# Turning the first feed-forward products: weights as the loaded operand, high and low token parts as one 512-column moving block

## The chip, the cores and the metric

The kernel runs on one core of one Trainium2 chip. A core has five engines that run side by side and meet only at semaphores: TensorE (PE, matrix products; its weight loads are listed apart as PEld), VectorE (DVE), ScalarE (ACT), GpSimd (POOL) and SyncE (SP, which here only issues transfers). A matrix product loads a 128 x up to 128 block into the array and lets up to 512 columns of another operand move through it; the sums land in PSUM, which has eight banks of 128 x 512 fp32. The metric is the device time of one execution in microseconds, the median of three runs. Less is better.

## The reference, cut to what matters

Two decoder blocks are applied to 256 tokens of width 1024, all in fp32. Between the mixers stand six feed-forward layers: two with a squared ReLU (hidden width 4096) and four gated ones (hidden width 2816).

```
def rms_norm(x, w):
    y = xf * lax.rsqrt(jnp.mean(xf * xf, axis=-1, keepdims=True) + NORM_EPS)
    return (y * w.astype(jnp.float32)).astype(x.dtype)

def squared_relu_mlp(h, w_up, w_down):
    return jnp.square(jax.nn.relu(h @ w_up)) @ w_down

def swiglu(h, w_in, w_out):
    gu = h @ w_in
    gate, up = jnp.split(gu, 2, axis=-1)
    return (jax.nn.silu(gate) * up) @ w_out
...
x = x + squared_relu_mlp(rms_norm(x, mlp_norm[layer]), w_up[layer], w_down[layer])     # twice
x = x + 0.5 * swiglu(rms_norm_2(x, ffn_norm[i, j]), ffn_w_in[i, j], ffn_w_out[i, j])   # four times
```

The factor rsqrt(...) of rms_norm is one number per token. It can be applied to the product `h @ w` afterwards.

## The kernel before, in words

**Products.** Every large product is done in three fp32r passes: an operand is split into a high part (rounded) and a low part (the rest), and high x high, high x low and low x high are summed in PSUM. The weights come from memory as panels of 128 x 2048 fp32 (1 MB) through a ring of four buffers `raw`; SP issues the load of panel q+4 when the low part of panel q has been made. ACT makes `w_hi` of a panel in two halves (`split`, L1427), DVE makes `w_lo` (L2001), in two buffers each. `multiply` (L611 to L613) is the three passes; it waits for `lo_ready` of each half panel, and counts `w_used` when a panel is done, which frees its buffers for the panel after the next.

**First feed-forward product before.** The transposed tokens `h_hi`, `h_lo` (128 of the 1024 inputs on the partitions, 256 tokens) are the loaded operand, in blocks of 128 tokens; 512 columns of weights move. So the result of a block of 512 hidden units has tokens on the partitions: two PSUM banks, one for each 128 tokens (`tt`). A block is two panels, thus 48 matmuls of 512 columns. There are 8 blocks in a squared-ReLU layer ("mlp"), 11 in a gated layer ("ffn"; a block is 256 gate and 256 up columns), 60 in all, with 2880 such matmuls.

**What follows a block.** ACT evacuates the banks with the token's norm factor `rstd` as a scale on the partition (L1483, ReLU; L1486, SiLU), DVE squares (L2064) or multiplies gate and up (L2070) into `tm`. The second product needs hidden units on the partitions, so PE transposes `tm` (`hidden_t`, `transpose_batch`, L625): 8 blocks of 128 x 128 for an mlp block, 4 for an ffn block, between the two panels of the next block. ACT and DVE split the transposed result into `hid_hi` (L1492) and `hid_lo` (L2077). The second product (`hid_hi`, `hid_lo` loaded, `w_down` moving) adds into `x_sb` (`residual`, L2034).

**Entering a layer.** `enter` does the first block in pieces: first half of panel 0, then `norm_batch` (transposes of the second half of `x_sb`, L625), second half, and after `t_lo` says that the second half of `h_lo` is there, panel 1. Meanwhile ACT sums squares (L1450) and POOL makes `rstd` (L2719, L2721); ACT goes on to the panels of block 1 only behind that.

The order on each engine is the order of the code; the loops over blocks (`Fori`) hold two blocks each before.

## Time and profile before

| | |
|---|---|
| time, median of 3 runs (lowest, highest) | 1735.3 us (1735.07, 1736.16) |
| profiled execution: its own time, its span | 1737.58 us, 1735.8 us |
| PE busy, PEld busy | 96%, 78% |
| DVE busy, ACT busy, POOL busy | 55%, 48%, 4% |
| mean granted TensorE clock | 0.99 |
| HBM | 167 GB/s over the span |

The three runs lie within 1.1 us. The time of an execution is 1.8 us more than its span (first to last recorded instruction). "Busy" of PE counts matmuls from their start to a modelled end, and they overlap: a 512-column matmul is listed with some 390 ns although the next begins 227 ns later. So what a matmul costs is read from the distance between starts, here called its pitch, or from the chain of waits, and not from its duration. For ACT and DVE, which work one instruction after another, the listed duration is the cost; two alike in a row are a little cheaper (a pair of DVE splits is 2.36 us, one alone 1.22).

### The profile page before, as it was taken

Reading aid. Unit: us, or ns where it says so; the run is one execution under the profiler, and the core shown is the slowest. Engines: PE = TensorE matmul, PEld = TensorE weight load, DVE = VectorE, ACT = ScalarE, POOL = GpSimd, SP = SyncE. Lnnn points to the kernel's source line nnn. Section 1 sums busy time; section 2 is a strip of 40 time slices with the busy share of each in tenths; the row PEclk is TensorE's granted clock in tenths of the full one; section 3 lists DMA queues with packets and bytes.
Section 4 is the critical chain, followed back from the end, with each engine's and each line's share of the span. In section 5 each row is a group of like instructions: output and inputs, shape, how many; then the busy total and the mean of one; then the engine's idle time right before and its main releaser. Section 6 shows DMA issues by size and latency. Waiting matters only on the chain.

```text
span 1735.8 us, 23226 instructions
## 1 busy us (share of the span) xinstructions
PE 1667.9 (96%) x8978; PEld 1359.5 (78%) x8978; DVE 962.3 (55%) x1250; ACT 840.4 (48%) x1213; POOL 75.5 (4%) x96
## 2 busy tenths in 40 slices
PE   6998999999999999799999999999999999899997
PEld 5778788887767888688888878888878888568886
DVE  4766565446765554455555565554555544465544
ACT  4742454344764543354445535444454435554433
POOL 1313000001000000000001000000000000000000
PEclk9999999999999999899999999999999999999999
DMA  7330444565213455445557544555545555235552
GB/s 260 127 117 22 175 170 170 197 220 223 98 50 128 172 185 194 157 171 189 176 199 270 177 148 185 191 174 193 212 162 182 194 195 193 73 122 193 185 193 83
DMA packets 41166, 291.75 MB, mean 168 GB/s; under 512 B 4832, under 2 KB 4992, under 8 KB 6528
## 3 DMA queue, kind: packets, MB, share of 16 engines
q1 hardware_dynamic: 39968, 282.75, 45.2%
q0 software_dynamic: 1120, 7.88, 1.4%
q8 instruction: 58, 0.95, 0.2%
q14 instruction: 20, 0.16, 0.0%
HBM read 289.56 MB, written 1.05 MB: 167 GB/s over the span
## 4 chain that ended last, share of the span: by engine, by line
PE 90%; DVE 5%; ACT 3%; issue 1%; DMA 0%; POOL 0%; SPq 0%; POOLq 0%; DVEq 0%; ACTq 0%
PE ps L611 26%; PE ps L613 25%; PE ps L612 25%; PE ps L625 3%; PE ps L965 2%; DVE w_lo L2001 1%; DVE gd_c L2304 1%; PE ps L777 1%; PE ps L778 1%; PE ps L779 1%; ACT w_hi L1427 1%; PE ps L1264 1%; DVE h_lo L2014 1%; PE ps L1250 0%; PE ps L842 0%
## 5 line engine op out<-in xcount | busy, mean ns | idle before, releaser
L2001 DVE TENSOR_TENSOR w_lo<-raw,w_hi 128x1024 fp32r<-128x1024 f32 x516 | 607.6, 1219 | 431.0 <-ACT w_hi L1427 427.1
L1427 ACT ACTIVATE w_hi<-raw 128x1024 fp32r<-128x1024 f32 x516 | 510.8, 1040 | 467.5 <-PE ps L613 442.2
L611 PE MATMUL ps<-w_hi,h_hi 128*128 128x512 f32 x1328 | 531.8, 400 | 16.6 <-DVE w_lo L2001 11.0
L613 PE MATMUL ps<-w_hi,h_lo 128*128 128x512 f32 x1328 | 520.9, 392 | 0.0
L612 PE MATMUL ps<-w_lo,h_hi 128*128 128x512 f32 x1328 | 520.1, 392 | 0.0
L611 PEld LDWEIGHTS ps<-w_hi,h_hi 128*128 128x128 f32 x1328 | 251.2, 189 | 73.7 <-issue 14.6
L613 PEld LDWEIGHTS ps<-w_hi,h_lo 128*128 128x128 f32 x1328 | 251.0, 189 | 53.9
L612 PEld LDWEIGHTS ps<-w_lo,h_hi 128*128 128x128 f32 x1328 | 251.6, 189 | 49.6 <-issue 0.5
L611 PE MATMUL ps<-w_hi,hid_hi 128*128 128x512 f32 x672 | 263.0, 391 | 0.0
L613 PE MATMUL ps<-w_hi,hid_lo 128*128 128x512 f32 x672 | 261.6, 389 | 0.0
L612 PE MATMUL ps<-w_lo,hid_hi 128*128 128x512 f32 x672 | 261.5, 389 | 0.0
L611 PEld LDWEIGHTS ps<-w_hi,hid_hi 128*128 128x128 f32 x672 | 126.2, 188 | 26.6 <-issue 0.9
L613 PEld LDWEIGHTS ps<-w_hi,hid_lo 128*128 128x128 f32 x672 | 126.1, 188 | 26.3
L612 PEld LDWEIGHTS ps<-w_lo,hid_hi 128*128 128x128 f32 x672 | 126.2, 188 | 25.6
L2077 DVE TENSOR_TENSOR hid_lo<-ps,hid_hi 128x512 f32 (+3 forms) x60 | 50.1, 834 | 151.6 <-ACT hid_hi L1492 151.6
L1492 ACT ACTIVATE hid_hi<-ps 128x512 f32 (+3 forms) x60 | 42.7, 712 | 188.7 <-PE ps L625 188.7
L1437 ACT ACTIVATE h_hi<-ps,norm_t 128x256 fp32r<-128x256 f32 x88 | 34.5, 475 | 70.1 <-PE ps L625 70.1
L2014 DVE SCALAR_TENSOR_TENSOR h_lo<-ps,norm_t,h_hi 128x256 fp32r<-128x256 f32 x88 | 36.5, 477 | 54.0 <-ACT h_hi L1437 54.0
L2719 POOL TENSOR_SCALAR ms<-ss 128x2 f32<-128x2 f32 x13 | 2.5, 191 | 1290.0 <-ACT junk L1450 1290.0
L625 PE MATMUL ps<-const,tm 128*128 128x128 f32 x304 | 42.9, 272 | 0.0
L625 PEld LDWEIGHTS ps<-const,tm 128*128 128x128 f32 x304 | 36.5, 140 | 8.0 <-DVE tm L2070 0.6
L2070 DVE SCALAR_TENSOR_TENSOR tm<-ps,rstd,tm 128x256 f32<-128x256 f32 x88 | 38.3, 477 | 2.2 <-ACT tm L1486 2.2
(302 smaller groups left out, 1164.7 us busy)
## 6 DMA issues: line engine op xcount, KB each, us to landing
raw<-in_stream SPq DMA_DIRECT2D x266, 1024.0 KB, 4.8
ns_w<-in_ns_w POOLq DMA_DIRECT2D x1, 4096.0 KB, 16.1
ln_rows<-in_ln_rows POOLq DMA_DIRECT2D x2, 1024.0 KB, 10.1
const<-in_const SPq DMA_DIRECT2D x1, 1044.0 KB, 14.3
x_sb<-in_x SPq DMA_DIRECT2D x2, 512.0 KB, 7.7
out<-x_sb SPq DMA_DIRECT2D x2, 512.0 KB, 3.1
row<-in_fin_rows SPq DMA_DIRECT2D x1, 512.0 KB, 18.8
row<-in_fin_rows POOLq DMA_DIRECT2D x1, 512.0 KB, 4.1
```

The costliest lines, as they stand in the source:

```text
L611: pe.matmul(bank[tt], a_hi[:, k_at + k, rows], hi, start=(k == 0), stop=False)
L612: pe.matmul(bank[tt], a_hi[:, k_at + k, rows], lo, start=False, stop=False)
L613: done = pe.matmul(bank[tt], a_lo[:, k_at + k, rows], hi, start=False, stop=(k == q.kt - 1))
L625: done = pe.transpose(tps[:, f, tt * P:(tt + 1) * P], src(tt, f), ident)
L965: done = pe.matmul(ps[half(c), bank, u * 64:(u + 1) * 64], lhs[half(c), u, :], rhs(c, u), start=(u == 0), stop=True, skip_group_check=True)
L1427: act.activation(w_hi[:, static % 2, part], raw[:, static % RING, part], ACT.Copy).then_inc(hi_ready, 1)
L1437: done = act.activation(h_hi[:, k, :], tps[:, f, :], ACT.Copy, scale=norm_t[:, n, k:k + 1])
L1492: act.activation(hid_hi2[:, bass.ds(b * (f_count * T), f_count * T)], tps[:, 0:f_count, :].rearrange("p f t -> p (f t)"), ACT.Copy).then_i ...
L2001: dve.tensor_tensor(w_lo[:, static % 2, part], raw[:, static % RING, part], w_hi[:, static % 2, part].bitcast(F32), ALU.subtract).then_inc ...
L2014: done = dve.scalar_tensor_tensor(h_lo[:, k, :], tps[:, f, :], norm_t[:, n, k:k + 1], h_hi[:, k, :].bitcast(F32), ALU.mult, ALU.subtract)
L2070: done = dve.scalar_tensor_tensor(gate, bank[tt][:, 256:512], rstd[:, tt:tt + 1], gate, ALU.mult, ALU.mult)
L2077: dve.tensor_tensor(hid_lo2[:, cols], tps[:, 0:f_count, :].rearrange("p f t -> p (f t)"), hid_hi2[:, cols].bitcast(F32), ALU.subtract).the ...
```

## The change

The first product of the six feed-forward layers is turned: `w_hi` and `w_lo` are loaded, and the tokens move. `h_hi` and `h_lo` become one buffer `h_both`, and for each 128 inputs (k) and each 128 hidden units (c) there are now two matmuls: `w_hi` loaded, 512 columns moving (256 tokens high, 256 tokens low), and `w_lo` loaded, 256 columns moving (high). A block is now one panel of 8 x 256 weights (256 hidden units; in ffn 128 gate and 128 up), so there are 16 blocks in an mlp layer and 22 in an ffn layer, 120 in all; the loops hold four. The result has hidden units on the partitions, and `hidden_t` is gone. ACT copies the low sums out of PSUM (`low_part`), DVE adds the high sums (`summed`) and applies the token factor, which now lies along the free axis: it is spread over the partitions once a layer, by POOL (two diagonal 128 x 128 blocks of `rstd`, `rms_diag`), PE (a 256-column product with `neg_ones` behind blocks 0 and 1) and ACT (`rows`, copy to `rms_row`). Squaring, or SiLU and the gate product (`gated`), write `inner`, which is split into `hid_hi` (ACT, `store`) and `hid_lo` (DVE, `low_part`). In ffn only the gate half is scaled before SiLU; the up half's factor is applied at the residual (`rstd_half`). The other hunks rename and merge semaphores, or repack the weights ahead of the launch.

```diff
+            def multiply_turned(q, b, bs, halves=(0, 1)):
+                panel = q.panel + b
+                slot = (q.panel + bs) % 2
+                bank = acc[(q.block + bs) % 2]
+                for s in halves:
+                    if s == 0:
+                        if bs >= 2:
+                            free, before, each = read[q.name]
+                            pe.wait_ge(free, before + each * (b - 1))
...
+                    pe.wait_ge(lo_ready, 2 * panel + s + 1)
+                    for k in range(4 * s, 4 * s + 4):
+                        for c in range(2):
+                            cols = slice(k * T + c * P, k * T + (c + 1) * P)
+                            pe.matmul(bank[c], w_hi[:, slot, cols], h_both[:, :, k, :], start=(k == 0), stop=False)
+                            done = pe.matmul(bank[c][:, 0:T], w_lo[:, slot, cols], h_hi[:, k, :], start=False, stop=(k == 7))
...
@@ enter, PE
                 pe.wait_ge(t_lo, t0 + 1)
+                if q.turned:
+                    multiply_turned(q, 0, 0, halves=(0,))
+                    norm_batch(layer, 1)
+                    multiply_turned(q, 1, 1, halves=(0,))
+                    pe.wait_ge(t_lo, t0 + 2)
+                    multiply_turned(q, 0, 0, halves=(1,))
+                    multiply_turned(q, 1, 1, halves=(1,))
+                    return
@@ hidden_layer, PE
-                def body(b, bs, i):
-                    multiply(up, b, bs, i, 0, h_hi, h_lo)
-                    hidden_t(b - 1)
-                    multiply(up, b, bs, i, 1, h_hi, h_lo)
+                pe.wait_ge(diag_ready, hidden_layers.index(layer) + 1)
+                pe.matmul(ps[:, 4, 0:T], cst("neg_ones"), rms_diag[:, :], start=True, stop=True).then_inc(tps_ready, 1)
+                turns, rest = steps(2, up.blocks)
+                with pe.Fori(0, turns) as i:
+                    for k in range(RING):
+                        multiply_turned(up, 2 + RING * i + k, 2 + k)
@@ hidden_layer, ACT
+                def low_part(b, bs):
+                    bank = 2 * ((up.block + bs) % 2)
+                    act.wait_ge(w_used, up.panel + b + 1)
...
+                    act.activation(tm[:, 0, :].rearrange("p (c t) -> p c t", t=T), two[bank][:, :, T:], ACT.Copy).then_inc(low_sums, 1)
+                def body(b, bs, i, weights):
+                    low_part(b - 1, bs - 1)
+                    weights((0,))
+                    if f_count == 1 and bs > 1:
+                        hidden(b - 1, bs - 1)
+                    weights((1,))
+                    if bs == 1:
+                        rows()
+                    if f_count == 2 or bs == 1:
+                        hidden(b - 1, bs - 1)
+                    store(b - 1, bs - 1)
@@ hidden_layer, DVE
+                def body(b, bs, i, weights):
+                    if bs >= 2:
+                        low_part(b - 2, bs - 2)
+                    summed(b - 1, bs - 1)
+                    if bs >= 2:
+                        scaled(b - 1, bs - 1)
+                        weights((0,))
+                    else:
+                        weights((0, 1))
+                        scaled(b - 1, bs - 1)
+                    if f_count == 1:
+                        gated(b - 1, bs - 1)
+                    if bs >= 2:
+                        weights((1,))
@@ inverse_rms, POOL
+                    pool.tensor_scalar(rstd_half[:, :], rstd[:, :], 0.5, None, ALU.mult)
+                    for tt in range(TT):
+                        done = pool.tensor_scalar(rms_diag[:, tt * P:(tt + 1) * P], ident, rstd[:, tt:tt + 1], -1.0,
+                                                  ALU.mult, ALU.mult)
```

PE, first mlp layer, block 1 into block 2 before: the end of panel 0 of block 1, the transposes of block 0's hidden units, and the start of panel 1.

```order
L611 MATMUL ps<-w_hi,h_hi 128x512
L612 MATMUL ps<-w_lo,h_hi 128x512
L613 MATMUL ps<-w_hi,h_lo 128x512
L625 MATMUL ps<-const,tm 128x128 [waits t_lo,tm_ready]
L625 MATMUL ps<-const,tm 128x128 x7
L611 MATMUL ps<-w_hi,h_hi 128x512 [waits lo_ready]
```

PE, the same layer after, the end of block 1 and the start of block 2:

```order
L652 MATMUL ps<-h_both,w_hi 128x512
L653 MATMUL ps<-h_both,w_lo 128x256
L713 MATMUL ps<-rms_diag,const 128x256 [waits diag_ready]
L716 UNCONDITIONAL_BRANCH
L716 ISA
L648 ISA [waits hid_sum]
L652 MATMUL ps<-h_both,w_hi 128x512 [waits lo_ready]
L653 MATMUL ps<-h_both,w_lo 128x256
```

The eight transposes are gone, three matmuls have become two, and one product for the token factors stands once a layer.

DVE, first mlp layer, between the norm's low parts (L2014) and the loop, before:

```order
L2014 SCALAR_TENSOR_TENSOR h_lo<-ps,norm_t,h_hi 128x256
L2001 TENSOR_TENSOR w_lo<-raw,w_hi 128x1024 [waits hi_ready] x4
L2064 TENSOR_TENSOR tm<-tm 128x1024 [waits act_tm]
L2077 TENSOR_TENSOR hid_lo<-ps,hid_hi 128x1024 [waits t_hi]
```

and after, up to the panel for block 3:

```order
L2077 SCALAR_TENSOR_TENSOR h_both<-ps,norm_t,h_both 128x256
L2140 TENSOR_TENSOR tm<-ps,tm 128x512 [waits low_sums]
L2064 TENSOR_TENSOR w_lo<-raw,w_hi 128x1024 [waits hi_ready] x2
L2147 SCALAR_TENSOR_TENSOR tm<-tm,rms_row 128x512 [waits hid_sum,rows_ready]
L2189 UNCONDITIONAL_BRANCH
L2189 ISA
L2161 ISA [waits t_hi]
L2161 TENSOR_TENSOR hid_lo<-inner,hid_hi 128x512
L2134 REGISTER_ALU
L2137 REGISTER_ALU [waits low_sums]
L2140 TENSOR_TENSOR tm<-ps,tm 128x512 [waits act_tm]
L2147 SCALAR_TENSOR_TENSOR tm<-tm,rms_row 128x512 [waits hid_sum]
```

Before, the splits of two panels stand first. After, the sum of block 0 stands ahead of the split of panel 2, and three steps (L2161, L2140, L2147) ahead of that of panel 3.

## Rows read from the trace of the kernel before

**Rows 1.** The page: granted TensorE clock in tenths, by slice of the span.
```profile
PEclk9999999999999999899999999999999999999999
```

**Rows 2.** The page: the chain that ended last, shares by engine.
```profile
PE 90%; DVE 5%; ACT 3%; issue 1%; DMA 0%; POOL 0%; SPq 0%; POOLq 0%; DVEq 0%; ACTq 0%
```

**Rows 3.** The chain in time order (start, us, what): transposes of two mlp blocks.
```profile
214.61 0.87 PE ps L625 x8
226.41 0.88 PE ps L625 x8
```

**Rows 4.** The chain in ffn00: transposes of two blocks.
```profile
747.72 0.44 PE ps L625 x4
759.09 0.44 PE ps L625 x4
```

**Rows 5.** Timeline, second mlp product (start, us, instruction): first and last of 22 matmuls.
```profile
300.15 0.39 PE L612 MATMUL ps<-w_lo,hid_hi 128*128 128x512 f32 x1
300.15 0.19 PEld L613 LDWEIGHTS ps<-w_hi,hid_lo 128*128 128x128 f32 x1
...
304.91 0.39 PE L612 MATMUL ps<-w_lo,hid_hi 128*128 128x512 f32 x1
```

**Rows 6.** Groups by line (busy us, mean ns, idle before): the hidden transposes.
```profile
L625 PE MATMUL ps<-const,tm 128*128 128x128 f32 x304 | 42.9, 272 | 0.0
```

**Rows 7.** Timeline: 24 fp32r matmuls of 256 columns, 48-column loads; first and last.
```profile
420.49 0.28 PE L1202 MATMUL ps<-h_hi,ns_wg_hi 128*48 128x256 f32 x1
...
423.11 0.28 PE L1204 MATMUL ps<-h_lo,ns_wg_hi 128*48 128x256 f32 x1
```

**Rows 8.** Timeline: the same with 16-column loads; first and last of 24.
```profile
41.51 0.28 PE L918 MATMUL ps<-h_hi,gd_wab_hi 128*16 128x256 f32 x1
...
44.20 0.28 PE L920 MATMUL ps<-h_lo,gd_wab_hi 128*16 128x256 f32 x1
```

**Rows 9.** Timeline: 16 loads of 128 columns for 32-column matmuls; the next load.
```profile
448.53 1.86 PEld L1230 LDWEIGHTS ps<-ns_kct,ns_qt 128*128 128x128 f32 x16 [0.76 <-issue]
...
450.31 0.19 PEld L611 LDWEIGHTS ps<-w_hi,h_hi 128*128 128x128 f32 x1
```

**Rows 10.** The chain in the spatial gating: eight fp32 matmuls of 256 columns.
```profile
1012.51 1.99 PE ps L734 x8
```

**Rows 11.** Groups: ACT and DVE work of the kinds that the change adds.
```profile
L2001 DVE TENSOR_TENSOR w_lo<-raw,w_hi 128x1024 fp32r<-128x1024 f32 x516 | 607.6, 1219 | 431.0 <-ACT w_hi L1427 427.1
L1427 ACT ACTIVATE w_hi<-raw 128x1024 fp32r<-128x1024 f32 x516 | 510.8, 1040 | 467.5 <-PE ps L613 442.2 <-POOL rstd L2721 11.0 <-PE ps L1075 10.8
...
L2070 DVE SCALAR_TENSOR_TENSOR tm<-ps,rstd,tm 128x256 f32<-128x256 f32 x88 | 38.3, 477 | 2.2 <-ACT tm L1486 2.2
...
L1874 ACT ACTIVATE ns_pt<-ps 128x512 f32<-128x512 f32 x24 | 13.8, 597 | 6.2 <-PE ps L1264 6.2
...
L2460 DVE TENSOR_TENSOR gd_xt<-gd_xt,ps 128x512 f32<-128x512 f32 x10 | 6.9, 688 | 3.5 <-PE ps L965 3.5
```

**Rows 12.** Timeline: the last matmul of a panel, and ACT's split that waits for it.
```profile
220.58 0.39 PE L613 MATMUL ps<-w_hi,h_lo 128*128 128x512 f32 x1
...
221.00 2.01 ACT L1427 ACTIVATE w_hi<-raw 128x1024 fp32r<-128x1024 f32 x2 [2.56 <-PE ps L613]
```

**Rows 13.** The chain entering mlp0: PE starts after a wait for DVE.
```profile
196.81 0.14 issue
196.95 0.47 PE ps L611
```

**Rows 14.** Timeline entering mlp0: DVE's split of panel 1, ACT behind rstd.
```profile
199.05 2.35 DVE L2001 TENSOR_TENSOR w_lo<-raw,w_hi 128x1024 fp32r<-128x1024 f32 x2
...
205.77 2.01 ACT L1427 ACTIVATE w_hi<-raw 128x1024 fp32r<-128x1024 f32 x2 [1.09 <-POOL rstd L2721]
```

**Rows 15.** Timeline entering ffn10: a 128 x 128 step of POOL.
```profile
1262.69 0.29 POOL L2847 CAST sb_eye<-const 128x128 bf16<-128x128 f32 x1
```

**Rows 16.** Timeline, first ffn block: ACT loads the SiLU table.
```profile
744.40 1.28 ACT L1486 ACT_TABLE_LOAD   x1
```

More of the change, by code:

```diff
@@ L67, in __init__ @@
         self.name, self.kt, self.blocks = name, kt, blocks
-        self.per = -(-kt // PK)
+        self.turned = name.endswith("_up")
+        self.per = 1 if self.turned else -(-kt // PK)
         self.panel, self.block = panel, block
@@ L531, in steps @@
         def steps(first, blocks):
[L534 to L535 removed]
+            turns = (blocks - first) // RING
+            return turns, first + RING * turns
         EV_ORDER = ((0, 0), (1, 0), (0, 1), (1, 1))
@@ L1475, in hidden_layer @@
                 t0 = at[layer][0] + 2
-                def evacuate(b, bs):
-                    act.wait_ge(w_used, up.panel + up.per * (b + 1))
-                    bank = acc[(up.block + bs) % 2]
-                    for tt in range(TT):
-                        if f_count == 4:
-                            done = act.activation(tm[:, tt, :], bank[tt], ACT.Relu, scale=rstd[:, tt:tt + 1])
-                        else:
-                            done = act.activation(tm[:, tt, 0:256], bank[tt][:, 0:256], ACT.Silu,
-                                                  scale=rstd[:, tt:tt + 1])
-                        done.then_inc(act_tm, 1)
@@ L1503, in hidden_layer, with rows @@
-                body(1, 1, 0)
-                pairs, rest = steps(2, up.blocks)
-                with act.Fori(0, pairs) as i:
-                    for k in range(2):
-                        body(2 + 2 * i + k, 2 + k, i)
-                for b in range(rest, up.blocks):
-                    body(b, b, 0)
+                h0 = hidden_before[layer]
+                n = hidden_layers.index(layer)
+                def rows():
+                    act.wait_ge(tps_ready, batches(layer) + 3)
+                    act.activation(rms_row[:, :], ps[:, 4, 0:T], ACT.Copy).then_inc(rows_ready, 1)
@@ new lines, in up_panel, with down_panel @@
+                def up_panel(b, bs, i):
+                    return lambda halves: split(up, b, bs, i, 0, halves)
+                def down_panel(j):
+                    return lambda halves: split(down, 0, 0, 0, j, halves)
+                body(1, 1, 0, up_panel(2, 2, 0))
+                turns, rest = steps(2, up.blocks - 1)
+                with act.Fori(0, turns) as i:
+                    for k in range(RING):
+                        body(2 + RING * i + k, 2 + k, i, up_panel(3 + RING * i + k, 3 + k, i))
@@ L1510, in hidden_layer @@
+                for b in range(rest, up.blocks - 1):
+                    body(b, b, 0, up_panel(b + 1, b + 1, 0))
+                for j in range(2):
+                    b = up.blocks - 1 + j
+                    body(b, b, 0, down_panel(j))
                 for b in range(down.blocks):
                     for j in range(down.per):
-                        if b == 0 and j == 2:
-                            evacuate(up.blocks - 1, up.blocks - 1)
-                            store_t(up.blocks - 1)
@@ L2024, in residual @@
                 q, b, scale = pending.pop()
+                layer = q.name.split("_")[0]
+                if layer in hidden_layers:
+                    dve.wait_ge(diag_ready, hidden_layers.index(layer) + 1)
                 if q.name in ("od_out", "sb_out") and b == 0:
@@ L2074, in store_t, with by_tile, summed @@
-                def store_t(b):
+                width = f_count * T
+                def by_tile(ap):
+                    return ap.rearrange("p (c t) -> p c t", t=T)
+                def summed(b, bs):
+                    bank = 2 * ((up.block + bs) % 2)
+                    dve.wait_ge(low_sums, h0 + b + 1)
+                    if f_count == 2:
+                        if not (isinstance(b, int) and b == 0) or h0:
+                            dve.wait_ge(act_tm, h0 + b)
+                    elif not (isinstance(b, int) and b == 0) or gated_before[layer]:
+                        dve.wait_ge(tm_ready, gated_before[layer] + b)
+                    dve.tensor_tensor(by_tile(tm[:, 1, :]), two[bank][:, :, 0:T], by_tile(tm[:, 0, :]), ALU.add).then_inc(hid_sum, 1)
@@ new lines, in up_panel, with down_panel @@
+                def up_panel(b, bs, i):
+                    return lambda halves: split(up, b, bs, i, 0, halves)
+                def down_panel(j):
+                    return lambda halves: split(down, 0, 0, 0, j, halves)
+                body(1, 1, 0, up_panel(2, 2, 0))
+                turns, rest = steps(2, up.blocks - 1)
+                with dve.Fori(0, turns) as i:
+                    for k in range(RING):
+                        body(2 + RING * i + k, 2 + k, i, up_panel(3 + RING * i + k, 3 + k, i))
@@ L2095, in hidden_layer @@
+                for b in range(rest, up.blocks - 1):
+                    body(b, b, 0, up_panel(b + 1, b + 1, 0))
+                for j in range(2):
+                    b = up.blocks - 1 + j
+                    body(b, b, 0, down_panel(j))
+                low_part(up.blocks - 1, up.blocks - 1)
                 for b in range(down.blocks):
                     for j in range(down.per):
-                        if b == 0 and j == 2:
-                            evacuate(up.blocks - 1, up.blocks - 1)
-                            store_t(up.blocks - 1)
```

238 lines of the change are left out of this document (125 added, 113 removed).

## The prediction

> **What bounds the kernel now.** I read the granted clock first: it is at the upper of its two levels, 2.4 GHz, in nearly every slice [rows 1], so PE times can be compared across the program. The chain of waits is 90% PE [rows 2]: what leaves PE's queue leaves the time, and what DVE and ACT do is free as long as PE does not wait for it.
>
> Then the pitch of matmuls, from starts in the timeline. In the second product 21 pitches take 304.91 - 300.15 = 4.76 us, 226.7 ns for 512 columns [rows 5]. An mlp block before is 48 of these and 8 transposes; it repeats every 226.41 - 214.61 = 11.80 us [rows 3]. 48 x 0.2267 = 10.88, so the transposes cost 0.92 us a block, of which 0.87 are their own (109 ns each) and the rest a slower start of the matmul behind them. An ffn block repeats every 759.09 - 747.72 = 11.37 us [rows 4]; its four transposes cost 11.37 - 10.88 = 0.49.
>
> **The change part by part.**
>
> *Transposes removed.* 304 of them [rows 6]. 16 mlp blocks x 0.92 + 44 ffn blocks x 0.49 = 14.7 + 21.6 = **-36.3 us**. All of it is on PE's own queue inside the chain, so it counts in full unless PE then waits for something.
>
> *Matmuls turned.* Before, 2880 matmuls of 512 columns. After, for each k and c one of 512 and one of 256: 120 blocks x 16 = 1920 pairs, 3840 loads. The columns are the same, 2880 x 512 = 1920 x 768. So the term is the pitch of a 256-column matmul with a load of its own of 128 columns, against half of 226.7. The trace has no such matmul in fp32r. Its neighbours: 256 columns with 48-column loads, 23 pitches in 2.62 us, 114 ns [rows 7]; with 16-column loads, 23 pitches in 2.69 us, 117 ns [rows 8]; and the load side alone, 128-column loads with tiny matmuls, (450.31 - 448.53)/16 = 111 ns [rows 9]. Moving and loading are thus nearly equal, 114 to 117 against 111. In the stream of 512 the next load begins with the running matmul (both at 300.15 [rows 5]), so I expect the longer of the two to set the pitch, and take 115.5, the middle of rows 7 and 8. Cost: 1920 x (226.7 + 115.5 - 1.5 x 226.7) = 1920 x 2.2 ns = **+4.1 us**. Ends: 111 ns gives -4.5 us. For the upper end I add to 106.7 (256 columns at 2.4 GHz) the 13.4 ns by which 226.7 exceeds 512 columns at 2.4 GHz, as if that were paid for each 128-column load: 120 ns, +12.8 us.
>
> *What the Trainium skill says against it.* The row first: in the 512 stream, load and matmul fit into 226.7 ns [rows 5], though a load takes 111 [rows 9] and the columns 213; a load is hidden there. The Trainium skill's page "TensorE: Matmul & The Clock Gate", Part 3 ("What overlaps and what doesn't"), says that a load overlaps a running matmul only when the row groups differ; here every load uses all rows. By that rule the 960 additional loads would stand bare. By that sentence the trace disagrees: it would want 213 + 111 = 324 ns. The first rival below is what is left of it.
>
> *Vector work per block.* A block is now 16 x (226.7 + 115.5) = 5.47 us of PE. DVE: `summed` and, in mlp, `scaled` and `low_part` at 0.69 each (128x512), two split halves at 1.22 [rows 11]: 3 x 0.69 + 2.44 = 4.51. In ffn three of 256 columns at 0.48 and one of 0.69: 4.57. ACT: `low_part` 0.60, halves 2.08, square and store 0.60 each: 3.88. Both fit under 5.47, but DVE has only 0.9 us left. The path that PE waits for: from the end of a block to ACT 0.19 us (220.58 + 0.227 against 221.00 [rows 12]), copy 0.60, `summed` 0.69, `scaled` 0.69, low half 1.22, and 0.14 to PE [rows 13], with 0.1 for handovers 3.6 us. PE asks for that half panel 5.47 us after the same moment. So 1.8 us are spare, and in the steady loop I charge **0**. Before, the split was all that stood there. The raw panels' transfers are freed a little later but four panels ahead, over 20 us: 0.
>
> *Entry of a layer.* Here the cover is thinner. I count from PE's first matmul of mlp0, 196.95 [rows 13]. First half of block 0 with the slow start: 2.96. Norm transposes 0.87: 3.83. Then first half of block 1, which needs the low half of panel 1: DVE begins it at 199.05, done at +3.32 [rows 14], early enough. It ends at 6.55; `t_lo` is waited for as before, and PE goes on at about 6.75 (the 48 matmuls ahead of 214.61 begin at 203.73 [rows 3]). Block 0 is done at 9.5, block 1 at 12.2. POOL: `rstd` is there at 8.8 [rows 14], the small step and two 128 x 128 steps at some 0.3 [rows 15] end by 10; no wait for `diag_ready`. The spread product is 1.99/8 = 0.25 us [rows 10]: 12.45. ACT begins the copy of block 0 at 9.7 (to 10.3), then the halves of panel 2 to 11.3 and 12.2. DVE sums to 11.0, and makes the low half from 11.3 to 12.5. PE goes on at 12.65 and pays 0.24 for a start after a wait (0.47 against 0.227 [rows 13]). Against an undisturbed 12.2: **0.7 us**.
> Block 2 then ends at 18.4. But DVE's order puts block 0's scale (13.7 to 14.3) behind both low halves, ACT squares and stores it by 15.6, and only then copies block 1 (16.2) and makes panel 3 (17.2). DVE: `low_part` to 16.3, `summed` 17.0, `scaled` 17.75, low half 19.0. PE needs it at 18.4: waits to 19.1, and 0.24: **1.0 us**. In ffn the steps are of 256 columns and save some 0.4 us; the table load (1.28 us [rows 16]) falls mostly into ACT's wait for the scale and costs 0.25: 0.8 us. Panel 4 comes in time. Sum: mlp 2 x 1.7, ffn 4 x 1.5 = **+9.4 us**. The bounds: 3 if the handovers come out better, 14 if each layer loses 0.8 more.
>
> *Small edits.* `rstd_half` and the wait in `residual`: the same instructions, factor ready long before; 0. The down product's first two panels are split in the loop's pattern instead of right away: same cover, 0.
>
> Sum: -36.3 + 4.1 + 9.4 = -22.8 us. Against its own profiled execution, span 1735.8 to 1713.0 (1714.8 with the 1.8 us around it); against the median of the runs 1735.3 - 22.8 = **1712.5 us**.
>
> **The rivals.**
>
> *A: the load does not hide under 256 columns (slower).* A load that needs 111 ns under 114 to 117 has 3 to 6 ns to spare. If any fixed handover between buffers is longer, part of each load shows, and from 1713 it takes (22.8/1920) = 12 ns a pair, a pitch above 127, to reach today's time. If the 960 additional loads stand in full: 960 x 0.111 = 106.6 instead of 4.1, thus 1712.5 + 102.5 = 1815 us. [...] For it: no row shows this pair, and a load is listed with 188 ns. Against: 16 loads follow each other at 111 ns in spite of their listed 190 [rows 9], and the transposes, which load 128 columns each, run at 109 [rows 3]. 5%.
>
> *B: the vector path sets the pace (slower).* If self-waits, register steps and SBUF traffic add over 0.9 us to DVE's 4.5 a block, or 1.8 us to the path, PE waits once a block, each time with 0.24 for the new start. At 0.3 us late it is 108 x 0.54 = 58 us: 1771. It decides at about 5.5 us of DVE per block; equality with today is at 0.2 us of wait in all for each block. 5%.
>
> *C: the pair at 120 ns, or entries twice as dear.* 1721 or 1722; both together 1731. Same sign, inside or at the edge of the range. 20%.
>
> *D: nothing given back*, pitch 111 to 113 and entries at 3 us: 1700 to 1704. 8%.
>
> That the transposes are not really gone is settled by the order of instructions: none of the 304 is left, and PE's queue has the 1920 pairs.
>
> **How the numbers follow.** Forecast 62%, D 8%, C 20%, A 5%, B 5%. The forecast's own range is 1706 to 1720; to hold 80% it takes in C but for its far end, and D's upper edge: 1703 to 1725. A measurement of this kernel tells 0.2%, 3.5 us, from no change. Slower by more: A and B less 2% for their mild forms, 8%. Within 0.2%: those 2%, and 2% for the far end of C (1731 and a little more), 4%. Faster: 88%.
>
> **What would show it.** In the profile after: 256-column matmuls (L653) starting 226.7 ns after the start of a L652, and the next L652 114 to 117 ns after them (step 2; 120 is C, over 127 is A). A block of 5.4 to 5.5 us and PE without idle time from block 4 on; DVE per block 4.5 us busy. If L652 shows idle time released by L2064 in every block, it is B. At each of six entries two short waits of PE on L2064, 0.4 and 0.8 us, and none on `diag_ready`. The chain should hold only the norm's transposes. I am wrong if the span moves by less than 15 or more than 35 us.

## The result and the profile after

The changed kernel takes 1724.5 us in the median of five runs (1722.38 to 1727.10), against 1735.3 (1734.40 to 1736.16, five runs): ratio 0.9939, 95% interval 0.9924 to 0.9953. It is faster by 10.8 us where 22.8 were forecast. The profiled execution has a span of 1722.7 us (1724.47 with what lies around it), 13.1 less than before where 22.8 were forecast. (The profiled execution of the kernel before, 1737.58 us, was 2.3 us above the median of its runs; that is the gap between 13.1 and 10.8.) A second measurement on another chip gave 1726.7 against 1736.6 us: 0.9944 (0.9927 to 0.9961).

The page after: the shares of PE and PEld, the chain by engine, and the two lines of the turned product (busy, mean ns, idle before).

```profile
PE 1653.2 (96%) x9646; PEld 1376.4 (80%) x9646; DVE 1077.1 (63%) x1534; ACT 924.1 (54%) x1399; POOL 81.3 (5%) x114
...
PE 88%; DVE 6%; ACT 4%; issue 1%; DMA 0%; POOL 0%; ACTq 0%; DVEq 0%; SPq 0%; POOLq 0%
...
L652 PE MATMUL ps<-h_both,w_hi 128*128 128x512 f32 x1920 | 677.0, 398 | 11.3 <-DVE h_both L2077 5.7
...
L653 PE MATMUL ps<-h_both,w_lo 128*128 128x256 f32 x1920 | 536.9, 280 | 0.0
```

The chain is still PE's for 88% (90% in [rows 2]), the 304 transposes [rows 6] are gone, and L652 has 11.3 us of idle time in all. So a wait in every block is not what is missing. The mean durations (398, 280) say nothing of the cost; the starts do. A "pair" is from here on one 512-column matmul with `w_hi` loaded and the 256-column one with `w_lo` loaded behind it. Timeline after, in the second half of mlp0's first product (first three rows: one pair and the start of the next; the last row is 99 pairs behind the first):

```profile
250.00 0.40 PE L652 MATMUL ps<-h_both,w_hi 128*128 128x512 f32 x1
250.23 0.28 PE L653 MATMUL ps<-h_both,w_lo 128*128 128x256 f32 x1
250.35 0.40 PE L652 MATMUL ps<-h_both,w_hi 128*128 128x512 f32 x1
...
284.98 0.40 PE L652 MATMUL ps<-h_both,w_hi 128*128 128x512 f32 x1
```

and in ffn00, the last row 203 pairs behind the first:

```profile
756.98 0.40 PE L652 MATMUL ps<-h_both,w_hi 128*128 128x512 f32 x1
757.21 0.28 PE L653 MATMUL ps<-h_both,w_lo 128*128 128x256 f32 x1
757.33 0.39 PE L652 MATMUL ps<-h_both,w_hi 128*128 128x512 f32 x1
...
827.36 0.39 PE L652 MATMUL ps<-h_both,w_hi 128*128 128x512 f32 x1
```

34.98/99 = 353.3 ns a pair in the one, 70.38/203 = 346.7 in the other, where equal columns at the old pitch [rows 5] would give 340.0 and the forecast had 342.2. Within a layer, from the fifth block on, the value is the same to a tenth of a nanosecond wherever one counts 48 pairs, whatever ACT and DVE do. It is one of two: 353.3 in mlp0, mlp1 and ffn11, 346.7 in ffn00, ffn01 and ffn10. Against 340.0 this is (256 + 256 + 352) x 13.3 + 3 x 352 x 6.7 = **+18.6 us**.

The starts also show where in the pair the time stands. Averaged from the fifth block of a layer on, the step from L652 to L653 is 236.0 ns at the upper value and 230.0 to 231.8 at the lower one, where the forecast had 226.7; the step from L653 to the next L652 is 117.4 and 114.9 to 116.7, inside the 114 to 117 that the forecast named as its sign, or 0.4 above. Most of the difference between the two values, and most of what is missing, stands behind the 512-column matmul.

Where the time went, layer by layer. The stretch runs from the start of the layer's second norm transposes to the start of the next transposes of the same kind behind it (in mlp1 and ffn11, which end a decoder block, to the start of DVE's last residual step); what a layer should have saved is its transposes (7.36 us in mlp, 5.39 in ffn, by [rows 3, 4]) less its pairs; the rest is the entry.

| layer | before, us | after, us | saved | transposes less pairs | entry |
|---|---|---|---|---|---|
| mlp0 | 152.5 | 149.5 | 3.0 | 7.36 - 3.41 | 0.9 |
| mlp1 | 180.5 | 177.6 | 2.9 | 7.36 - 3.41 | 1.1 |
| ffn00 | 169.7 | 167.8 | 1.9 | 5.39 - 2.35 | 1.1 |
| ffn01 | 169.7 | 167.9 | 1.8 | 5.39 - 2.35 | 1.3 |
| ffn10 | 169.7 | 167.3 | 2.4 | 5.39 - 2.35 | 0.6 |
| ffn11 | 184.1 | 184.5 | -0.4 | 5.39 - 4.69 | 1.1 |

Sum: 11.7 us saved in these stretches, 6.1 spent on entries; the other 1.4 us of the 13.1 lie outside them. 1.2 of these are there before mlp0's stretch begins (198.52 after, 199.76 before). They need not be an effect of the change: when the changed kernel was profiled again, the same stretch began at 199.89. The entry's wait, in PE's timeline after, at block 3 of mlp0 and of mlp1 (in brackets: idle before, and who ended it):

```profile
214.56 0.50 PE L652 MATMUL ps<-h_both,w_hi 128*128 128x512 f32 x1 [0.56 <-DVE w_lo L2064]
...
548.85 0.50 PE L652 MATMUL ps<-h_both,w_hi 128*128 128x512 f32 x1 [0.50 <-DVE w_lo L2064]
```

Ffn00, ffn01 and ffn11 have the same wait with 0.35, 0.46 and 0.46 us; ffn10 has none, and block 2 waits for `w_lo` in no layer. What leads to it, in the chain of mlp0 after (start, us, what):

```profile
205.82 1.06 ACT w_hi L1465
206.90 0.98 DVE w_lo L2064
...
209.18 0.69 DVE tm L2147
209.90 0.64 ACT inner L1533
...
211.10 0.59 ACT tm L1527
...
211.97 0.69 DVE tm L2140
...
213.29 1.23 DVE w_lo L2064
214.52 0.04 issue
214.56 0.50 PE ps L652
```

This is the order that the prediction walked through (scale, square, copy of block 1, sum, low half). Counted from PE's first matmul of the layer, now 195.62, the low half is done at 18.9; the forecast had 19.0. PE's slow start behind it is 0.50 us, as the 0.47 of [rows 13].

### The profile page after: what moved, and what is told of

Read it like the earlier page. It is cut to its first block, busy times and chain, and to the rows that moved or that the text cites. A ratio compares the mean times of both kernels' runs of the same rounds, so it can differ in the third digit from the quotient of the medians.

```text
span 1722.7 us, 25805 instructions
## 1 busy us (share of the span) xinstructions
PE 1653.2 (96%) x9646; PEld 1376.4 (80%) x9646; DVE 1077.1 (63%) x1534; ACT 924.1 (54%) x1399; POOL 81.3 (5%) x114
## 4 chain that ended last, share of the span: by engine, by line
PE 88%; DVE 6%; ACT 4%; issue 1%; DMA 0%; POOL 0%; ACTq 0%; DVEq 0%; SPq 0%; POOLq 0%
PE ps L652 25%; PE ps L627 13%; PE ps L629 13%; PE ps L628 13%; PE ps L653 12%; DVE w_lo L2064 2%; PE ps L1002 2%; PE ps L664 1%; DVE gd_c L2405 1%; ACT w_hi L1465 1%; PE ps L814 1%; PE ps L816 1%; PE ps L815 1%; PE ps L1301 1%; DVE h_both L2077 1%
## 5 line engine op out<-in xcount | busy, mean ns | idle before, releaser
L652 PE MATMUL ps<-h_both,w_hi 128*128 128x512 f32 x1920 | 677.0, 398 | 11.3 <-DVE h_both L2077 5.7
L653 PE MATMUL ps<-h_both,w_lo 128*128 128x256 f32 x1920 | 536.9, 280 | 0.0
L652 PEld LDWEIGHTS ps<-h_both,w_hi 128*128 128x128 f32 x1920 | 361.0, 188 | 101.4 <-DVE h_both L2077 7.6
L653 PEld LDWEIGHTS ps<-h_both,w_lo 128*128 128x128 f32 x1920 | 362.8, 189 | 0.0
L2140 DVE TENSOR_TENSOR tm<-ps,tm 128x512 f32<-128x512 f32 x120 | 83.0, 692 | 162.3 <-ACT tm L1527 162.3
L1527 ACT ACTIVATE tm<-ps 128x512 f32<-128x512 f32 x120 | 71.6, 596 | 187.5 <-PE ps L653 178.0
L627 PE MATMUL ps<-w_hi,h_both 128*128 128x512 f32 x368 | 150.7, 410 | 7.7 <-DVE w_lo L2064 7.7
L629 PE MATMUL ps<-w_hi,h_both 128*128 128x512 f32 x368 | 145.3, 395 | 0.0
L628 PE MATMUL ps<-w_lo,h_both 128*128 128x512 f32 x368 | 145.2, 395 | 0.0
L627 PEld LDWEIGHTS ps<-w_hi,h_both 128*128 128x128 f32 x368 | 70.4, 191 | 25.4 <-issue 10.6
L629 PEld LDWEIGHTS ps<-w_hi,h_both 128*128 128x128 f32 x368 | 70.2, 191 | 15.3
L628 PEld LDWEIGHTS ps<-w_lo,h_both 128*128 128x128 f32 x368 | 70.6, 192 | 14.2 <-issue 0.8
## 6 DMA issues: line engine op xcount, KB each, us to landing
row<-in_fin_rows SPq DMA_DIRECT2D x1, 512.0 KB, 18.6
```

Of the source, the lines that this page charges most:

```text
L627: pe.matmul(bank[tt], a_hi[:, k_at + k, rows], hi, start=(k == 0), stop=False)
L628: pe.matmul(bank[tt], a_hi[:, k_at + k, rows], lo, start=False, stop=False)
L629: done = pe.matmul(bank[tt], a_lo[:, k_at + k, rows], hi, start=False, stop=(k == q.kt - 1))
L652: pe.matmul(bank[c], w_hi[:, slot, cols], h_both[:, :, k, :], start=(k == 0), stop=False)
L653: done = pe.matmul(bank[c][:, 0:T], w_lo[:, slot, cols], h_hi[:, k, :], start=False, stop=(k == 7))
L1527: act.activation(tm[:, 0, :].rearrange("p (c t) -> p c t", t=T), two[bank][:, :, T:], ACT.Copy).then_inc(low_sums, 1)
```

## The experiments

Two theories stand against each other for the missing 14.5 us: that the pair itself is dearer (and why: the load (L), the two pieces of the moving block (S), ACT and DVE beside it (V), or the order (O)), and that the vector path or the entries took it.

### The pitches by themselves

PE alone, on ready data, streams of 128 matmuls of a line (shortened: the line is repeated for k and c):

```diff
+ matmul(512, w_hi[128 cols], two pieces);  matmul(256, w_lo[128 cols], h)      # L101, L102
+ matmul(512, w_hi[128 cols], one piece);   matmul(256, w_lo[128 cols], h)      # L106, L107
+ 512, 512, 256, 256                                                            # L111, L113
+ 256, 256 with loads of 128 (L117, L118), of 64 (L122, L123)
+ 512, 256 with loads of 64 (L127, L128), of 96 (L132, L133); 64, 64 with loads of 128 (L137, L138)
+ 512, 384 with loads of 128 (L142, L143)
```

> Only TensorE works here, on ready data: the reference's computation is left out altogether. Each line is a stream of 128 fp32r matmuls of one kind, so the distance between starts is that kind's pitch. In the changed kernel a pair (512 columns behind a load of w_hi, 256 behind a load of w_lo) takes 346.7 or 353.3 ns instead of the 1.5 x 226.7 = 340.0 of equal columns. Theory L (the load of 128 columns is not quite hidden under 256 moving columns): both pair lines, with the tokens in two pieces or in one, show 347 to 353; the pair with loads of 64 or 96 columns shows 340 or less; 256 columns alone with 128-column loads 116 to 127 a matmul, with 64-column loads less. Theory S (the 512 moving columns lie in two pieces 8 KB apart): the pair in two pieces 347 to 353, the pair in one piece 340; 512 in two pieces above 227. Theory V (DVE and ACT, which write and read SBUF and PSUM beside it, slow it): every pair 340 here. Theory O (512 and 256 columns alternate): high, high, low, low gives another time than high, low, high, low.

Timeline of this kernel: the first matmul of each stream, so that the difference of two starts over the number of matmuls is the pitch.

```profile
193.90 0.39 PE L101 MATMUL ps<-h_both,w_hi 128*128 128x512 f32 x1
...
239.11 0.40 PE L106 MATMUL ps<-h_con,w_hi 128*128 128x512 f32 x1
...
284.34 0.63 PE L111 MATMUL ps<-h_con,w_hi 128*128 128x512 f32 x2
...
328.92 0.28 PE L117 MATMUL ps<-h_con,w_hi 128*128 128x256 f32 x1
...
359.64 0.28 PE L122 MATMUL ps<-h_con,w_hi 128*64 128x256 f32 x1
...
388.66 0.39 PE L127 MATMUL ps<-h_con,w_hi 128*64 128x512 f32 x1
...
432.19 0.39 PE L132 MATMUL ps<-h_con,w_hi 128*96 128x512 f32 x1
...
477.42 0.19 PE L137 MATMUL ps<-h_con,w_hi 128*128 128x64 f32 x1
```

Two pieces: 45.21/128 = 353.2 ns a pair; one piece: 45.23/128 = 353.4. Order by k: 44.58/128 = 348.3. 256 columns alone: 30.72/256 = **120.0**; with loads of 64 columns 29.02/256 = 113.4. The pair with loads of 64: 43.53/128 = 340.1; with loads of 96: 45.23/128 = 353.4. Loads of 128 behind 64 columns: 111.7 each until 483.37; behind that the granted clock is 0.50, the lower level, and they take 213.3. So the load matters, as theory L says: a load takes 111.7 ns by itself, 256 columns with a short load take 113.4, but the two together take 120.0, not the longer of the two. One line of L missed: with loads of 96 the pair was to show 340 or less, and shows 353.4. (A short load also fills fewer rows of PSUM; these streams don't part the two. That 512 columns with short loads get no faster, below, speaks for the load.) S falls (the pair costs the same in one piece and in two, and 512 columns in two pieces take 226.7), V falls (353 with ACT and DVE idle), O is right in part: the order moves the pair between 348 and 353.

One more stream bears on L. The pair of 512 and 384 columns, at the upper clock again, 84 pairs apart:

```profile
545.76 0.39 PE L142 MATMUL ps<-h_con,w_hi 128*128 128x512 f32 x1
...
579.92 0.39 PE L142 MATMUL ps<-h_con,w_hi 128*128 128x512 f32 x1
```

34.16/84 = 406.7 ns a pair, 6.6 above the sum of 226.7 and the 173.4 that 384 columns take alone (below). There the load of 111.7 has 160 ns of moving columns to hide behind. So mixed lengths can cost 6.7 ns more than their parts although no load is short of room, and the upper value, 353.3 = 226.7 + 120.0 + 6.7, has the same excess. It is one stretch; whether this pair has a lower value too was not tried.

### The moving block in one piece

```diff
- h_both = sb("h_both", [P, 2, DK, T], F32R)
+ h_both = sb("h_both", [P, DK, 2, T], F32R)
```

> The changed kernel with h_both laid out so that the 512 moving columns (high and low tokens of one k) lie in one piece. Theory S: pair 340.0 ns in all layers, 864 x 13.3 + 1056 x 6.7 = 18.6 us less than the changed kernel, some 1706 us. Theories L, V and O: pairs stay at 346.7 or 353.3, 1724 within 3 us.

1728.5 us (1725.4 to 1731.8), beside 1726.7 for the changed kernel on the same chip. No gain beyond the scatter; its layers show 353.3, 353.3, 346.7, 353.3, 346.7, 353.3.

### The order by k

```diff
-  for c in range(2): matmul(high, c); matmul(low, c)
+  for c in range(2): matmul(high, c)
+  for c in range(2): matmul(low, c)
```

> The changed kernel with the matmuls of one k in the order high c0, high c1, low c0, low c1. Theory O (alternating lengths, or two matmuls in a row into one bank, cost the step): 340 ns a pair, 18 us less, some 1706 us. Theory L: two short matmuls in a row now each have a load of the next behind them; one load in two lies under 256 columns as before, so no change, or, if the loads may run ahead by one, a change of at most 6.7 ns a pair, 13 us. Theories S and V: no change, 1724 within 3 us.

1720.9 us (1720.28 to 1722.24), ratio 0.9907 (0.9891 to 0.9924). Not the 18 us of theory O, but 5.8 us less than the changed kernel on the same chip. 348.3 ns a pair in every layer, against a mean of 349.7 in the first profile of the changed kernel and of 349.1 in the one beside it: that accounts for 1.5 to 2.6 us. Of the 4.6 us between the two profiled spans, 1.7 lie in the six stretches of the table and 2.9 outside them; the latter I can't explain. Two executions of the changed kernel alone differ by 1.4 us before mlp0's stretch begins, so a part of it may be scatter.

### The changed kernel again

> The changed kernel once more. If the pair's pitch is set by the program alone, each layer shows the same pitch as in the first profile: 353.3, 353.3, 346.7, 346.7, 346.7, 353.3 ns. If it settles anew in each execution (on one of two steps of 6.67 ns), other layers show 353.3, and a layer of 352 pairs moves by 2.35 us; that would explain times that spread over 4.7 us where the kernel before spreads over 1.8.

1726.7 us. Now mlp0, mlp1, ffn00 and ffn01 have 346.7 and ffn10 and ffn11 353.3. The program was the same, so the value is settled in each execution. The layers move with it: mlp0's stretch is 148.2 us (149.5 in the first profile: 1.3 less, 1.7 expected), ffn10's 169.4 (167.3: 2.1 more, 2.3 expected).

### Other lengths, longer groups, and ten starts

> TensorE alone again, all of the reference's computation left out: streams of fp32r matmuls, 96 of a line, with other lengths and other loads. So far: 512 columns 226.7 ns, 256 columns 120.0, both 13.3 over their columns at 2.4 GHz, with loads of 128 columns; 256 columns with loads of 64 113.4, 6.7 over. Theory F (each load of 128 columns costs its matmul a fixed 13.3 ns, whatever moves): 384 columns 173.3, 192 columns 93.3 or the load's own 111.7; 512 with loads of 64 columns 220.0; a pair of which only one load is short 346.7 or less. Theory G (the load runs in parallel and only the longer of the two counts): 384 at 166.7, 512 with short loads still 226.7. Then ten times the same 96 pairs, each after a wait of PE for ACT and after 0 to 4 matmuls of 256 columns: if the pair's pitch is settled at the start of a stretch, each of the ten holds one value, 346.7 or 353.3, and both occur; if it belongs to the program alone, all show 353.3. Groups of 1, 2, 4 and 8 k (high products first, then low ones): 348.3 for 1, and nearer to 346.7 the longer the group.

Timeline: the first matmul of four of the streams (96 of each line).

```profile
195.23 0.34 PE L116 MATMUL ps<-h_con,w_hi 128*128 128x384 f32 x1
...
228.52 0.25 PE L121 MATMUL ps<-h_con,w_hi 128*128 128x192 f32 x1
...
249.93 0.42 PE L126 MATMUL ps<-h_con,w_hi 128*128 128x512 f32 x1
...
283.25 0.39 PE L131 MATMUL ps<-h_con,w_hi 128*64 128x512 f32 x1
...
315.91 0.63 PE L139 MATMUL ps<-h_con,w_hi 128*128 128x512 f32 x2
```

384 columns: 33.29/192 = 173.4, again 13.3 over the columns at 2.4 GHz. 192 columns: 21.41/192 = 111.5, the load's own time. 256 columns with loads of 96: 116.0. 512 columns with loads of 64 or 96: 230.0, not less but more than 226.7, so F is wrong as "a fixed price per load"; G is wrong there and on 384 columns (166.7 expected). The two half-short pairs (L126 and L127, then L131 and L132) decide which load counts. Short load for the 256-column matmul, full load for the 512: 33.32/96 = 347.1 ns. The other way round: 32.66/96 = 340.2. The load that costs is the full one of `w_hi`, which runs while the 256 columns move; shortening that of `w_lo`, behind 512 columns, gains nothing against the lower value. Each of the two streams ran once, so whether 347.1 has an upper value beside it isn't shown. Groups of 1, 2, 4 and 8 k: 348.3, 350.8, 349.2 and some 348 ns a pair; longer groups don't come nearer to 346.7, though that was expected. Of the ten stretches of alternating pairs, nine held 353.3 and one 346.7.

### Which mixtures have two values

> TensorE alone, all of the reference's computation left out: 38 stretches of 192 fp32r matmuls (96 pairs), each after a wait for ACT of another length. Ten of alternating pairs, ten in the order by k (two of 512, two of 256), six of 256 columns alone, six of 512 alone, six of pairs whose 512-column matmul has a load of 64 columns. Theory: the second value of the pitch belongs to 128-column loads behind a 256-column matmul that stands between longer ones: the ten pairs show both 346.7 and 353.3 (so far 9 of 10 the upper one), the order by k 348.3 in all ten, 256 alone 120.0 in all, 512 alone 226.7 in all, the pairs with the short load of w_hi 340.2 in all. Rival (any mixture can fall on two values by its start): the order by k and the short load vary from stretch to stretch as well.

Timeline: first and last L99 and first and last L108, two of the ten stretches of pairs; first and last are 95 pairs apart.

```profile
33.77 0.39 PE L99 MATMUL ps<-h_con,w_hi 128*128 128x512 f32 x1
...
67.32 0.40 PE L99 MATMUL ps<-h_con,w_hi 128*128 128x512 f32 x1
...
68.22 0.50 PE L108 MATMUL ps<-h_con,w_hi 128*128 128x512 f32 x1 [0.38 <-ACT spare L59]
...
101.26 0.39 PE L108 MATMUL ps<-h_con,w_hi 128*128 128x512 f32 x1
```

33.55 us and 33.04 us for the same work; the second has a slower first start (0.1 us) within it. Of the ten, four held 353.3 and six 346.7. The ten stretches by k took 32.83 to 32.87 us (from the first two long matmuls to the last two, 94 pairs), the six of 256 alone 22.88 to 22.90, the six of 512 alone 43.19 to 43.24, the six with a short load of `w_hi` 32.37 to 32.38: one value each. So the second value belongs to the alternating pair, and goes when the load of `w_hi` is cut to 64 columns, as the theory had it. That it needs a 256-column matmul is not shown: loads of 96 gave 353.4, and 512 with 384 columns has the same excess. Two equal lengths in a row are enough to be rid of it.

### The removed term by itself

The kernel before with one transpose a block; the other 244 are left out.

```diff
-  for tt in range(TT):
-      for f in range(f_count):
-          done = pe.transpose(tps[:, f, tt * P:(tt + 1) * P], src(tt, f), ident)
+  pe.transpose(tps[:, f_count - 1, P:], tm[:, 1, (f_count - 1) * P:f_count * P], ident)
```

> The kernel before with only the last of the 8 (or 4) transposes of each block of hidden units; the other 244 are left out, so the second products get stale numbers for them. It measures the removed term by itself: at 109 ns each 26.6 us less, 1709 to 1710 us; the remaining 60 and their slower starts make up 9.7 us of the 36.3. If the transposes were partly hidden, less.

1709.9 us beside 1736.0: 26.1 less, ratio 0.9852 (0.9836 to 0.9869), where 26.6 were expected. An mlp block repeats every 11.03 us in its profile, an ffn block every 11.02: 0.15 and 0.14 over the 10.88 of 48 matmuls [rows 5], for the one transpose that is left and the slower start behind it. So the -36.3 stand.

### Room in the vector work

```diff
+  if bs >= 2: dve.tensor_tensor(extra[:, 0, :], h_hi[:, 0:2, :], h_lo[:, 0:2, :], ALU.add)   # once, or twice
```

> The changed kernel with one additional DVE step of 128 x 512 on SBUF (0.69 us by the rows of that shape) at the head of every block from the second on, its result unused. By the prediction DVE has 4.5 us of work a block and PE 5.47 (now 5.55 to 5.65), and the path to the low half panel 3.6: with 0.69 more 5.2 and 4.3, both still below, so no change in the steady loop, and at the entries up to 2 x 0.69 x 6 = 8 us. Theory 'the vector path has no room' (what the forecast lost went there): PE waits in every block, over 108 x 0.5 = 54 us more.

> The same with two additional steps: DVE 4.5 + 1.4 = 5.9 us a block against 5.55: the bound moves to DVE, 0.35 us and a new start of PE (0.24) in each of some 108 blocks, 40 to 65 us more: 1765 to 1790. This is the point from which the second rival decides.

1733.0 us (1729.7 to 1736.0) with one step and 1738.7 (one run) with two, on a chip where the kernel before takes 1737.1. PE's waits for the low part, in the list of waits (us in total, times, longest) of the first, then the second:

```profile
PE ps L653 <- DVE w_lo L2065: 8.8, 8, 2.0
```

```profile
PE ps L653 <- DVE w_lo L2065: 12.4, 8, 2.0
```

The changed kernel has the same row with 5.6 us, seven times. Eight waits, not 108: even two additional steps leave the steady loop without a wait. What they cost in waits falls on the entries, 3.2 and 6.8 us; the pairs add to it (with two steps five of six layers held 353.3, 4.7 us more than in the first profile). My expectation for two steps, 40 to 65 us, was wrong. Ffn00, 70 us of steady loop with two steps (window, length, busy us of PE, PEld, DVE, ACT and POOL, clock, DMA share, GB/s), and below DVE's steps within it:

```profile
765.00:835.00 70.00, 70.00 (x399) 60.74 (x398) 66.64 (x102) 41.97 (x64) 0.00 (x0) 1.00 0.53 194
```

```profile
769.29 0.69 DVE L2170 TENSOR_TENSOR extra<-h_both 128x512 f32<-128x512 f32 x1
769.89 0.68 DVE L2171 TENSOR_TENSOR extra<-h_both 128x512 f32<-128x512 f32 x1
770.49 0.68 DVE L2141 TENSOR_TENSOR tm<-ps,tm 128x512 f32<-128x512 f32 x1
```

DVE is at 66.64 of 70 us, at its limit but not over it. Steps that wait for nothing start 0.60 us apart though each is listed with 0.68 or 0.69: each starts before the one ahead has ended. So an additional step costs 0.6, and a block of the changed kernel needs 4.2 us of DVE (52.88 busy us in the same 70), not 4.57.

### High products first, at first with the old wait and then without it

```diff
-  pe.wait_ge(lo_ready, 2 * panel + s + 1)
+  pe.wait_ge(hi_ready, 2 * panel + s + 1)          # the first of the two kernels keeps lo_ready here
   for k in range(4 * s, 4 * s + 4): for c in range(2): matmul(high, k, c)
+  pe.wait_ge(lo_ready, 2 * panel + s + 1)
+  for k in range(4 * s, 4 * s + 4): for c in range(2): matmul(low, k, c)
```

> The changed kernel with all eight high products of a half panel first, then its eight low products; PE waits for the low part at the start of the half as before. If a pair can't be under 226.7 + 120.0 = 346.7 and the step of 6.7 falls once in 16 matmuls instead of once in each pair: 347.1 a pair in every layer, against 349.7 in the mean of the first profile: 1920 x 2.6 = 5 us less than the changed kernel, 1719 to 1720, with runs that lie closer together. If the step comes from the change of length itself, once per change: the same figure. If it comes from the load (each short matmul pays it): 1720.9 as with the order by k, or up to 1726.

> The same order, and PE waits only for w_hi before the eight high products, and for w_lo before the low ones, 8 x 226.7 = 1.8 us later. Theory E (at each of six entries the wait is for w_lo, 0.9 to 1.3 us and a fresh start): 6 us in all, of which at least 4 go: 1713 to 1715 us. Rival (ACT's chain is what is late at the entries, so w_hi is late too): less than 1.5 us below the kernel with the same order.

With the old wait 1722.3 us (1721.8 to 1723.2), above the 1719 to 1720 expected: 2.793 us for half a panel, 349.2 ns a pair in all layers, and not 347.1. So the excess is not paid once per group or once per change of length; of the three theories only the one by which each short matmul pays has 1722.3 in its range. Waiting for `w_hi` alone: 1719.5 (1718.3 to 1720.3), ratio 0.9905 (0.9889 to 0.9922), 2.8 us less, between theory and rival. The chain of mlp0 there, from the norm's transposes on:

```profile
202.00 2.07 PE ps L652 x8
204.07 0.95 PE ps L657 x8
205.02 1.84 PE ps L652 x8
206.86 0.95 PE ps L657 x8
207.81 0.43 PE ps L717 x2
208.25 1.85 PE ps L652 x8
210.09 0.95 PE ps L657 x8
211.04 1.84 PE ps L652 x8
212.88 0.95 PE ps L657 x8
213.84 1.84 PE ps L652 x8
```

Block 3 (213.84) no longer waits. Five of the six stretches are shorter than those with the old wait by 0.6 to 0.8 us: the 0.42 to 0.52 us of the wait there and some 0.27 of the slower start behind it, so the mechanism is as theory E says. Its 4 to 6 us were too many, since the entries' 6.1 us are only in part such waits: the spreading product takes 0.43 us a layer and stays. Ffn10, which had no wait to lose, is 0.5 us longer, and PE's timeline shows why:

```profile
1256.85 1.42 PE L652 MATMUL ps<-h_both,w_hi 128*128 128x512 f32 x5 [0.42 <-DVE h_both L2081]
```

The layer's first product no longer waits 2.03 us for `w_lo` but 0.79 for `w_hi`, before the stretch begins. PE then comes 1.2 us sooner to the second half of `h_both`, and waits for that instead, which it did not do before.

### Both together

Blocks 0 to 3 of a layer with high products first, all later ones in the order by k.

> The changed kernel with both findings: blocks 0 to 3 of a layer in the order high products first, waiting only for w_hi before them, and all later blocks in the order by k (high c0, high c1, low c0, low c1), which measured 348.3 ns a pair in all layers against 349.2 with eight and eight. 1476 pairs (four blocks of 16 pairs fewer in each of six layers, 1920 - 384 = 1536, and a few at the loop's end) x 0.9 = 1.4 us less than with high products first everywhere (1719.5): 1718. If the loop's start brings the waits back (block 4 too is late): up to 1720.

1717.2 us (1716.8 to 1719.0), ratio 0.9890 (0.9873 to 0.9906): 19.9 us less than the kernel before on its chip, where the changed kernel's two measurements gave 10.8 and 9.9, and the best version found. It keeps the change; only PE's order and one wait differ (and blocks 2 and 3 stand ahead of the loop). That it ends in the forecast's range is luck as far as the forecast goes: neither step was in it.

## Why the prediction was right and wrong

**Transposes, -36.3: right.** 244 of the 304 taken away alone gave 26.1 of 26.6 us.

**The pair, +4.1: wrong, and this is the step that failed.** It came to +18.6 in the first profile. The forecast said that the longer of moving and loading sets the pitch of the 256-column matmul, took 115.5 ns for it, the middle of the rows with 16- and 48-column loads [rows 7, 8], and left the 512-column matmul beside it at 226.7 without a reason. In streams of one length, 256 columns take 113.4 ns with loads of 64, 116.0 with 96 and 120.0 with 128, while the load alone takes 111.7: the longer of the two is not what comes out, and a row with a shorter load is no stand-in. (The 117 ns of rows 8, with loads of 16, don't fit into that order; why is open.) In the pair itself the 256-column matmul is followed after 114.9 to 117.4 ns, much as forecast, and most of what is missing stands behind the 512-column one: 230.0 to 231.8 or 236 instead of 226.7. The sum at the lower value, 346.7, is that of the two lengths alone, 226.7 + 120.0, and case C's +12.8; the forecast had it as a bound and not as the value. The second value, 353.3, was in no case: 864 pairs x 6.7 = 5.8 us more.

**Rival A: wrong in size, right in place.** The loads are not bare: of 111 ns, 6.7 show (or 13.3). 512 columns run at 226.7 with full loads of all rows in the turned form as well. So the rule weighed in the prediction (the Trainium skill, "TensorE: Matmul & The Clock Gate", Part 3, "What overlaps and what doesn't": a load overlaps only where row groups differ) agrees with no stream here. By that sentence and the figures of this case the pair would take, as an estimate, 213 + 107 + 2 x 111 = 542 ns; the prediction's 1815 us charges only the 960 additional loads, while the rule leaves all 3840 bare, and those of the kernel before as well.

**Vector work, 0 in the steady loop: right**, with more room than I gave it: 4.2 us a block instead of 4.57, and two more steps fit. The forecast summed listed durations; back to back they overlap.

**Entries, +9.4: half of the mechanism right, size too high.** Block 3 waits as forecast and from the chain that the forecast walked, 0.5 us and 0.27 of slow start (forecast 1.0; in ffn 0.8). Block 2 does not: its low half is there in time, and the place costs, in mlp0, the spreading product's 0.34 us and 0.11 of a slower start, not 0.7. The six entries came to 6.1 us, within the bounds of 3 and 14. No wait on `diag_ready`, as said.

**The sum.** -36.3 + 18.6 + 6.1 - 1.4 = -13.1, the change of the span. The forecast missed by 9.7: 14.5 on the pairs, -3.3 on the entries, -1.4 elsewhere (the parts rounded). "Wrong if the span moves by less than 15" applies: it moved 13.1. By the medians of the runs it moved 10.8. The direction held, and the range (1703 to 1725) with 0.5 us to spare in the first measurement; the second (1726.7) lies above it. One sum of the prediction is off: by its own prices, case D (pitch 111 to 113, entries at 3 us) gives 1697.5 to 1701, not 1700 to 1704.

**What stays open.** What in the start of a stretch decides between 346.7 and 353.3, and why mixed lengths cost more than their parts. Some pitches are multiples of 6.67 ns (226.7 is 34 of them, 120.0 is 18, 346.7 is 52, 353.3 is 53), others are not (348.3, 349.2, 230.0, 116.0), and the single steps inside a pair are not either. So no fixed grid of starts follows from these runs.

## What to carry to other kernels

When a change halves the columns behind each load, don't price the new matmul with a row whose load is shorter: when moving and loading are about equal, add what the long matmuls show over their columns, and measure the mixture itself, since it can cost more than its parts. Group equal lengths (two long, then two short) rather than alternate them: 348.3 ns lies above the alternating pair's lower value, but it is the same each time. Let the products that need only the high part go first, so that the wait for the low part stands behind 1.8 us of work. Room on a vector engine is best measured by adding a step: the sum of listed durations was 9% too high here.

## What the runs showed of the hardware

- A pair of a 512- and a 256-column fp32r matmul, each with a full load, runs at 346.7 or at 353.3 ns, and keeps the value for a whole stretch of 96 to 288 pairs. In 22 stretches of PE alone (2, 10 and 10 in the three kernels) it was the upper in 15 and the lower in 7; in the layers of the two profiles of the changed kernel the upper in 5, the lower in 7. Whether the runs scatter more for it isn't shown: in the first measurement the kernel before spreads over 1.8 us and the changed kernel over 4.7, in the second over 4.9 and 3.3.
- Most of the excess of the pair stands in the step from the 512- to the 256-column matmul: 236.0 ns at the upper value and 230.0 to 231.8 at the lower, against 226.7 in a stream of 512 alone. The pair of 512 and 384 columns takes 406.7, against 400.1 for its parts.
- 512 columns with loads of 64 or 96 columns take 230.0 ns, with loads of 128 226.7. The shorter load made it slower.
- With loads of 96 columns the pair ran at the upper value (353.4, one stretch), with loads of 64 it loses the whole excess (340.1).
